# Where the attention masks are added: an identity product on TensorE, or an addition by VectorE in PSUM

## The chip, the cores and the metric

One NeuronCore of a Trainium2 chip runs the whole program. The metric is the device time of one execution in microseconds. It was 2264.13 us as the median of three runs (2263.20 to 2264.96).

## The reference

The input is one sequence of 256 tokens with 1024 features. Two blocks of two layers each follow one another. All arithmetic is fp32. What matters here are the attentions, each of which masks its scores before a softmax:

- Block 1, per layer: a sliding-window attention with sinks, 8 query heads over 2 shared key heads of 64 columns:

```
scores = jnp.where(valid[None, :, None, None], scores, -jnp.inf)
sink = jnp.broadcast_to(sinks..., scores.shape[:-1] + (1,))
probs = jax.nn.softmax(jnp.concatenate([scores, sink], axis=-1), axis=-1)[..., :-1]
```

- Block 2, per layer: a causal latent attention (8 heads, 96 columns per key), and a sparse attention with three branches (compressed keys, selected keys, window) of 8 heads over 2 key heads each:

```
s = jnp.einsum('bthd,bshd->bhts', qi, k).astype(jnp.float32) * scale
s = jnp.where(kpos[None, :] <= qpos[:, None], s, NEG_INF)
p = jax.nn.softmax(s, axis=-1).astype(v.dtype)
```

With 256 tokens all 4 blocks of 64 keys are selected, and the window of 512 covers everything, so that both of those branches are plain causal attentions. A cross-attention of 4 heads per layer has no mask. Block 1 also has a stick-breaking attention, whose mask the change does not touch. The rest are projections, gates and feed-forward products.

## The kernel before

**Products.** Each fp32 product is made from three passes over rounded halves: a weight piece of 1024 columns lands in a ring of 7 slots (SyncE issues the DMA, L380), ScalarE rounds it to `w_high` (L401), VectorE subtracts to get `w_low` (L404), and TensorE multiplies high by high, high by low and low by high. In `gemm_beside` (L602, L603) two instructions do that for 128 features and 256 tokens; one such *gate tile* uses up one weight piece. VectorE then adds the two halves of the bank (L612), and ScalarE applies the gate function (L1462 or L2222). PSUM banks 0 to 3 serve these products.

**Attention units.** The heads of an attention are worked off in units that fill one PSUM bank, 4 or 5 in turn. For query tile t the width of a head is 128 * (t + 1) keys (16 in the compressed branch), and a unit has up to 512 columns. So each attention has, per layer, two units of 4 heads for t = 0 and four units of 2 heads for t = 1; the compressed branch has four units of 4 heads. A unit passes through four engines' instructions:

1. `scores` or `scores_of_two` on TensorE: the mask by an identity product, and a product for each head (L916 or L893); flag `scored`.
2. `maximum` on VectorE: the row maximum (L1036), in block 1 the maximum with the sink (L1044), and its negative (L1040, in block 1 L1048); flag `max_ready`.
3. `exponentials` on ScalarE: for each head an exponential out of the bank (L1090) and a read of the row sum (ACTIVATION_READ_ACCUMULATOR on the same line); flag `p_ready` with the last.
4. `turn_weights` on TensorE: four transposes (L935) into bank 6, after `p_ready` and after the copy of the unit before; `copy` on VectorE (L1059); `values` on TensorE (L951) into bank 7.

**The mask.** It lies in SBUF as bf16, 0 or -1e30. Where a head is 256 wide and `mask_late` is set (all of block 2), the left 128 keys are allowed anyway, so the product only adds the causal triangle to the right half of each head, after the scores (L898, L923; 256 columns). Everywhere else it opens the bank (L888, L911): 512 columns, or 64 in the compressed branch.

**The order beside it** is written out by hand, the same for all engines. The window attention of block 1 and the sparse attention of block 2 are taken two units at a time (`attend_tensor_by_two`, `attend_vector_by_two`): scores of units u and u + 1, values of u - 2, a gate tile or branch product, transposes of u, values of u - 1, another product, transposes of u + 1. VectorE takes both maxima, then the sum of a finished product, a weight piece's `w_low`, the copy of u, and so on. The latent attention is taken one unit at a time (`attend_tensor`): scores of u, transposes of u - 1, one or two gate tiles, values of u - 2. Here VectorE has, between two maxima, one or two gate sums, as many weight pieces, and a slice of side work from a generator (rotations at L1138 to L1144, the short convolution at L2557 to L2575). ScalarE has the weight pieces of the next products (L401) right behind the exponentials of a unit. On each engine the instructions run in the order they are written.

Of the kernel before, what the change touches and what calls it, by code (L numbers as in the profile page):

```python
# [8 lines left out]
ALU = mybir.AluOpType  # L9
# [3 lines left out]
P = 128  # L13
# [262 lines left out]
class Core:  # L276
# [600 lines left out]
    def scores(self, pe, l, u):  # L877
# [5 lines left out]
        region = bank[:, 0:len(heads) * w]  # L883
        mask = a["mask"](t)
        late = mask is not None and w == 2 * P and a["mask_late"]
        started = mask is not None and not late
        if started:
            pe.matmul(region, self.identb[:, :], mask[:, 0:len(heads) * w], start=True, stop=False,  # L888
                      skip_group_check=True)
# [6 lines left out]
        if late:  # L896

            m = pe.matmul(region.rearrange("p (h w) -> p h w", w=w)[:, :, P:w], self.identb[:, :],  # L898
                          self.masks[:, 0, 0:len(heads) * P], start=False, stop=True, skip_group_check=True)
        m.then_inc(*self.flag("scored").one())  # L900

    def scores_of_two(self, pe, l, u):
# [5 lines left out]
        w, mask, late = a["width"](t), a["mask"](t), a["mask_late"] and a["width"](t) == 2 * P  # L908
        if not late:
            for bank, _, _, heads in both:  # L910
                pe.matmul(bank[:, 0:len(heads) * w], self.identb[:, :], mask[:, 0:len(heads) * w], start=True,  # L911
                          stop=False, skip_group_check=True)
        for i in range(len(heads)):
            for bank, _, _, heads in both:
                (q, k), = a["qk"](heads[i], t)
                m = pe.matmul(bank[:, i * w:(i + 1) * w], q, k, start=late and i == 0, stop=True,  # L916
                              skip_group_check=True)
                if not late and i == len(heads) - 1:
                    m.then_inc(*self.flag("scored").one())
        if late:  # L920
            for bank, _, _, heads in both:
                region = bank[:, 0:len(heads) * w].rearrange("p (h w) -> p h w", w=w)
                pe.matmul(region[:, :, P:w], self.identb[:, :], self.masks[:, 0, 0:len(heads) * P], start=False,  # L923
                          stop=True, skip_group_check=True).then_inc(*self.flag("scored").one())
# [104 lines left out]
    def vector_steps(self, dve, l, us, names, finishes):  # L1029
        def maximum(u):  # L1030
# [4 lines left out]
            src = self.psum[:, 4 + u % 2, 0:len(heads) * w].rearrange("p (h w) -> p h w", w=w)  # L1035
# [2042 lines left out]
```

## Time and profile before

| | |
|---|---|
| median of 3 runs | 2264.13 us |
| the profiled execution, its own time | 2265.73 us |
| its span | 2264.0 us |
| ScalarE busy | 1121.6 us (50%) |
| GpSimd busy | 202.4 us (9%) |
| chain that ended last: PE, DVE, ACT, DMA | 96%, 2%, 1%, 1% |
| TensorE clock granted, mean | 0.998 of full |

The span runs from the first to the last instruction that the hardware profiler recorded; the device time has a little around it. In the timeline view each row has a start, a length, the engine, the line and the operation; "[1.93 <-ACT w_high L401]" says that the engine had been idle for 1.93 us and that this instruction released it. TensorE's rows overlap: a matmul's length includes its way through the array, so what it costs the next one is read from start to start. VectorE's rows overlap by some 0.08 us as well when one does not wait for the other.

### The profile page before, as it was taken

The numbers are of one execution on the slowest core, as the hardware profiler recorded it, in microseconds if no ns is written. First come the engines' busy times: TensorE is split into PE (matmuls) and PEld (weight loads), VectorE is DVE, ScalarE is ACT, GpSimd is POOL, SyncE is SP. The second block draws the span as 40 slices with busy tenths as digits, with TensorE's granted clock in tenths as the row PEclk, the third lists the DMA queues.
The fourth block names the chain that finished last, engine by engine and source line by source line (L and its number), as shares of the span: only waits on it lengthen the run. The fifth ranks groups of instructions, "written<-read, shape, count | busy, mean of one in ns | idle before, by whom it ended". The sixth has DMA issues, their size and how long they took to land.

```text
span 2264.0 us, 33433 instructions
## 1 busy us (share of the span) xinstructions
PE 2240.2 (99%) x13314; PEld 1936.3 (86%) x13314; DVE 1552.8 (69%) x2158; ACT 1121.6 (50%) x1737; POOL 202.4 (9%) x192
## 2 busy tenths in 40 slices
PE   8999999999999999999999999999999999999998
PEld 7898888888888888788889988888888888998887
DVE  5677855667864775677777677577655777777764
ACT  4645444554543544545454554454445545455543
POOL 0001200001210210000004001011100000220110
PEclk9999999999999999999999999999999999999999
DMA  6335565434555655554435455565556544364554
GB/s 234 127 134 185 187 203 179 149 122 155 202 192 185 226 193 190 171 184 154 168 103 168 168 205 186 188 222 185 188 172 188 170 154 136 122 214 167 187 191 135
DMA packets 108987, 395.61 MB, mean 175 GB/s; under 512 B 12374, under 2 KB 12544, under 8 KB 108576
## 3 DMA queue, kind: packets, MB, share of 16 engines
q1 hardware_dynamic: 104256, 377.01, 49.7%
q0 software_dynamic: 4576, 16.45, 2.2%
q8 instruction: 107, 1.75, 0.3%
q14 instruction: 48, 0.39, 0.0%
HBM read 392.92 MB, written 1.05 MB: 174 GB/s over the span
## 4 chain that ended last, share of the span: by engine, by line
PE 96%; DVE 2%; ACT 1%; DMA 1%; issue 0%; SPq 0%; DVEq 0%; ACTq 0%
PE psum L447 43%; PE psum L603 28%; PE psum L602 14%; PE psum L951 3%; PE psum L818 2%; PE psum L935 1%; PE psum L916 1%; PE psum L893 1%; PE psum L2039 1%; DMA ring<-in_weights 1%; DVE w_low L404 1%; PE psum L1310 0%; PE psum L1298 0%; DVE x L680 0%; DVE xs L2409 0%
## 5 line engine op out<-in xcount | busy, mean ns | idle before, releaser
L404 DVE TENSOR_TENSOR w_low<-ring,w_high 128x1024 fp32r<-128x1024 f32 x704 | 858.6, 1231 | 351.7 <-ACT w_high L401 349.8
L603 PE MATMUL psum<-xT,w_high 128*128 128x512 f32 x2784 | 980.2, 395 | 0.0
L401 ACT ACTIVATE w_high<-ring 128x1024 fp32r<-128x1024 f32 x704 | 734.6, 1056 | 476.8 <-DMA ring<-in_weights 476.1
L602 PE MATMUL psum<-xT,w_low 128*128 128x256 f32 x2784 | 788.8, 283 | 0.1
L603 PEld LDWEIGHTS psum<-xT,w_high 128*128 128x128 f32 x2784 | 523.0, 188 | 119.1
L602 PEld LDWEIGHTS psum<-xT,w_low 128*128 128x128 f32 x2784 | 526.8, 189 | 1.3 <-issue 0.4
L447 PE MATMUL psum<-w_high,hidden 128*128 128x512 f32 x1216 | 376.9, 390 | 0.0
L447 PEld LDWEIGHTS psum<-w_high,hidden 128*128 128x128 f32 x1216 | 228.2, 188 | 47.2
L447 PE MATMUL psum<-w_low,hidden 128*128 128x512 f32 x608 | 236.6, 389 | 0.0
L447 PE MATMUL psum<-w_high,xT 128*128 128x512 f32 (+2 forms) x640 | 193.2, 383 | 3.7 <-ACT xT L771 1.4
L447 PE MATMUL psum<-rounded_pages,w_high 128*128 128x256 f32 x896 | 165.1, 286 | 0.0
L623 POOL TENSOR_TENSOR hidden<-attn_pT,hidden 128x256 fp32r<-128x256 f32 (+1 forms) x108 | 111.1, 1029 | 580.6 <-ACT hidden L2153 390.2
L447 PEld LDWEIGHTS psum<-w_high,xT 128*128 128x128 f32 x640 | 119.5, 190 | 30.4 <-issue 9.6
L447 PEld LDWEIGHTS psum<-rounded_pages,w_high 128*128 128x128 f32 x896 | 139.4, 191 | 0.5
L447 PEld LDWEIGHTS psum<-w_low,hidden 128*128 128x128 f32 x608 | 114.1, 188 | 23.5
L612 DVE TENSOR_REDUCE attn_p<-psum 128x256 f32<-128x512 f32 x136 | 93.8, 690 | 55.9 <-PE psum L603 54.2
L1090 ACT ACTIVATE attn_p<-psum,nmx 128x256 f32<-128x256 f32 (+2 forms) x176 | 68.3, 401 | 128.4 <-DVE nmx L1040 100.1
L447 PE MATMUL psum<-rounded_pages,w_low 128*128 128x256 f32 x448 | 126.7, 283 | 0.0
L447 PE MATMUL psum<-w_high,rounded_pages 128*128 128x512 f32 x384 | 123.8, 395 | 0.0
L447 PE MATMUL psum<-w_low,xT 128*128 128x512 f32 (+2 forms) x320 | 120.0, 380 | 0.0
L2173 ACT ACTIVATE attn_p<-attn_p 128x256 f32<-128x256 f32 x80 | 33.4, 418 | 136.3 <-DVE attn_p L612 136.2
L612 DVE TENSOR_REDUCE attn_pT<-psum 128x256 f32<-128x512 f32 x80 | 55.3, 691 | 61.8 <-PE psum L603 61.7
(245 smaller groups left out, 2197.4 us busy)
## 6 DMA issues: line engine op xcount, KB each, us to landing
ring<-in_weights SPq DMA_DIRECT2D x706, 512.0 KB, 3.5
pages<-in_affine POOLq DMA_DIRECT2D x16, 512.0 KB, 5.7
ring<-in_weights SPq DMA_DIRECT2D x8, 440.0 KB, 3.1
pages<-in_gains POOLq DMA_DIRECT2D x4, 512.0 KB, 5.1
pages<-in_mem POOLq DMA_DIRECT2D x2, 1024.0 KB, 5.5
ring<-in_weights SPq DMA_DIRECT2D x4, 384.0 KB, 3.1
pages<-in_rows POOLq DMA_DIRECT2D x2, 512.0 KB, 5.9
y<-x SPq DMA_DIRECT2D x4, 256.0 KB, 2.0
```

What stands on the lines that cost most here:

```text
L401: eng.activation(high, raw, ACT.Copy).then_inc(self.flag("w_rounded").sem, 1)
L404: eng.tensor_tensor(self.w_low[:, piece % SLOTS, 0:width], raw, high.bitcast(F32), ALU.subtract).then_inc(self.flag("w_split").sem, 1)
L447: m = pe.matmul(out, a, b, start=(first and i == 0), stop=(last and i == len(pairs) - 1))
L602: pe.matmul(out[:, 0:SEQ], low, self.xT_high[:, k, :], start=(k == 0), stop=False, skip_group_check=True)
L603: m = pe.matmul(out, high, self.xT[:, k, :, :].rearrange("p x s -> p (x s)"), start=False, stop=(k == kn - 1), skip_group_check=True)
L612: dve.tensor_reduce(out, h.rearrange("p (x s) -> p s x", x=2), AX, ALU.add).then_inc(*self.drained(banks, key))
L623: pool.tensor_tensor(low, whole[:, n % (4 // tiles), :], high.bitcast(F32), ALU.subtract).then_inc(*self.flag("hidden").one())
L818: m = pe.transpose(out, src, self.ident[0:n, 0:n])
L893: m = pe.matmul(bank[:, i * w:(i + 1) * w], q, k, start=not started, stop=True, skip_group_check=True)
L951: m = pe.matmul(self.psum[:, 7, h * dv:(h + 1) * dv], self.attn_pT[0:n, u % 2, c * P:(c + 1) * P], a["v"](h, kt), start=(kt == 0), stop=(k ...
L1090: m = act.activation(self.attn_p[:, u % 2, i * w:(i + 1) * w], self.psum[:, 4 + u % 2, i * w:(i + 1) * w], ACT.Exp, bias=self.nmx[:, t, h: ...
L2173: act.activation(silu[:, n % 4, :], silu[:, n % 4, :], ACT.Silu).then_inc(*c.flag("silu").one())
```

## The change

The identity products go; the scores of the first head open the bank instead. VectorE adds the mask to the same columns of the bank in place, ahead of the row maximum, and the maximum waits for it. The `scored` flag is now set by the last score product of each unit. The expected totals of the flag `dve_step` rise by 6 and 22 per layer, one for each masked unit.

```diff
 def scores(self, pe, l, u):
-        region = bank[:, 0:len(heads) * w]
-        mask = a["mask"](t)
-        late = mask is not None and w == 2 * P and a["mask_late"]
-        started = mask is not None and not late
-        if started:
-            pe.matmul(region, self.identb[:, :], mask[:, 0:len(heads) * w], start=True, stop=False,
-                      skip_group_check=True)
+        started = False
...
-        if late:
-            m = pe.matmul(region.rearrange("p (h w) -> p h w", w=w)[:, :, P:w], self.identb[:, :],
-                          self.masks[:, 0, 0:len(heads) * P], start=False, stop=True, skip_group_check=True)
         m.then_inc(*self.flag("scored").one())
...
 def scores_of_two(self, pe, l, u):
-        if not late:
-            for bank, _, _, heads in both:
-                pe.matmul(bank[:, 0:len(heads) * w], self.identb[:, :], mask[:, 0:len(heads) * w], start=True,
-                          stop=False, skip_group_check=True)
...
-                if not late and i == len(heads) - 1:
+                if i == len(heads) - 1:
                     m.then_inc(*self.flag("scored").one())
-        if late:
-            for bank, _, _, heads in both:
-                region = bank[:, 0:len(heads) * w].rearrange("p (h w) -> p h w", w=w)
-                pe.matmul(region[:, :, P:w], self.identb[:, :], self.masks[:, 0, 0:len(heads) * P], start=False,
-                          stop=True, skip_group_check=True).then_inc(*self.flag("scored").one())
...
 def maximum(u):
             src = self.psum[:, 4 + u % 2, 0:len(heads) * w].rearrange("p (h w) -> p h w", w=w)
+            if a["mask"](t) is not None:
+                late = w == 2 * P and a["mask_late"]
+                masked = src[:, :, P:w] if late else src
+                mask = (self.masks[:, 0, 0:len(heads) * P] if late else a["mask"](t)[:, 0:len(heads) * w]
+                        ).rearrange("p (h w) -> p h w", h=len(heads))
+                dve.tensor_tensor(masked, masked, mask, ALU.add).then_inc(*self.flag("dve_step").one())
+                self.settle(dve, l, "dve_step")
             dve.tensor_reduce(self.mx[:, t, hs], src, AX, ALU.max
                               ).then_inc(*self.flag("dve_step").one())
```

**VectorE, first two units of the window attention (block 1, layer 0).** `psum` is the bank of scores, `mx` and `nmx` the maximum and its negative, `w_low` a weight piece, `fac` the sinks' term. Before:

```order
L404 TENSOR_TENSOR w_low<-ring,w_high 128x1024
L1036 TENSOR_REDUCE mx<-psum 128x4
L1044 SCALAR_TENSOR_TENSOR mx<-mx,rows 128x4
L1048 TENSOR_SCALAR nmx<-mx 128x4
L1036 TENSOR_REDUCE mx<-psum 128x4
L1044 SCALAR_TENSOR_TENSOR mx<-mx,rows 128x4
L1048 TENSOR_SCALAR nmx<-mx 128x4
L994 TENSOR_TENSOR fac<-nmx,rows 128x8
```

With the change:

```order
L404 TENSOR_TENSOR w_low<-ring,w_high 128x1024
L1021 TENSOR_TENSOR psum<-psum,masks 128x512
L1023 TENSOR_REDUCE mx<-psum 128x4
L1031 SCALAR_TENSOR_TENSOR mx<-mx,rows 128x4
L1035 TENSOR_SCALAR nmx<-mx 128x4
L1021 TENSOR_TENSOR psum<-psum,masks 128x512
L1023 TENSOR_REDUCE mx<-psum 128x4
L1031 SCALAR_TENSOR_TENSOR mx<-mx,rows 128x4
L1035 TENSOR_SCALAR nmx<-mx 128x4
L974 TENSOR_TENSOR fac<-nmx,rows 128x8
```

One addition stands ahead of each maximum, behind the same weight piece; nothing else moved.

**VectorE, latent attention (block 2, layer 0), units 1 and 2.** The rows between the two maxima are unit 0's copy, two gate sums, two weight pieces and the side work. Before:

```order
L1036 TENSOR_REDUCE mx<-psum 128x4
L1040 TENSOR_SCALAR nmx<-mx 128x4
L1059 COPY attn_pT<-psum 128x512
L612 TENSOR_REDUCE gates<-psum 128x256 x2
L404 TENSOR_TENSOR w_low<-ring,w_high 128x1024 x2
L2557 TENSOR_TENSOR pages<-pages,cols 128x15x16 x2
L1036 TENSOR_REDUCE mx<-psum 128x2
L1040 TENSOR_SCALAR nmx<-mx 128x2
```

With the change:

```order
L1021 TENSOR_TENSOR psum<-psum,masks 128x512
L1023 TENSOR_REDUCE mx<-psum 128x4
L1027 TENSOR_SCALAR nmx<-mx 128x4
L1046 COPY attn_pT<-psum 128x512
L612 TENSOR_REDUCE gates<-psum 128x256 x2
L404 TENSOR_TENSOR w_low<-ring,w_high 128x1024 x2
L2544 TENSOR_TENSOR pages<-pages,cols 128x15x16 x2
L1021 TENSOR_TENSOR psum<-psum,masks 128x2x128
L1023 TENSOR_REDUCE mx<-psum 128x2
L1027 TENSOR_SCALAR nmx<-mx 128x2
```

The copy, the gate sums and the weight pieces come after the first addition, and the second unit's mask has 256 columns.

**TensorE, latent attention, scores of unit 2 and transposes of unit 1.** Before:

```order
L602 MATMUL psum<-xT,w_low 128x256
L603 MATMUL psum<-xT,w_high 128x512
L893 MATMUL psum<-pages 128x256 x2
L898 MATMUL psum<-masks,identb 128x2x128
L935 MATMUL psum<-ident,attn_p 128x128 x4
```

With the change:

```order
L602 MATMUL psum<-xT,w_low 128x256
L603 MATMUL psum<-xT,w_high 128x512
L887 MATMUL psum<-pages 128x256 x2
L915 MATMUL psum<-ident,attn_p 128x128 x4
```

The identity product that stood ahead of the transposes is gone, and the transposes follow the scores directly.

## Rows read from the trace of the kernel before

**Rows 1.** The page: busy time of each engine and its share of the span.
```profile
PE 2240.2 (99%) x13314; PEld 1936.3 (86%) x13314; DVE 1552.8 (69%) x2158; ACT 1121.6 (50%) x1737; POOL 202.4 (9%) x192
```

**Rows 2.** Timeline of TensorE: start, length, then the instruction; mask products and what follows.
```profile
120.44 0.60 PE L911 MATMUL psum<-masks,identb 128*128 128x512 bf16 x2
120.98 1.16 PE L916 MATMUL psum<-pages 64*128 64x128 f32 x16
...
1050.80 0.39 PE L888 MATMUL psum<-masks,identb 128*128 128x512 bf16 x1
1051.03 1.06 PE L893 MATMUL psum<-pages 96*128 96x128 f32 x8
...
1065.55 0.28 PE L898 MATMUL psum<-masks,identb 128*128 128x256 bf16 x1
1065.66 0.64 PE L935 MATMUL psum<-ident,attn_p 128*128 128x128 f32 x4
...
1119.91 0.23 PE L911 MATMUL psum<-masks,identb 128*128 128x64 bf16 x2
1120.08 1.07 PE L916 MATMUL psum<-kcmpT,pages 64*128 64x16 f32 x16
```

**Rows 3.** VectorE's groups by form: count | busy us, mean ns | idle before, releaser.
```profile
L1553 DVE TENSOR_TENSOR x<-x,psum 128x512 f32<-128x512 f32 x16 | 10.9, 682 | 6.1 <-PE psum L447 6.1
...
L2591 DVE TENSOR_TENSOR pages<-pages,psum 128x256 f32<-128x256 f32 x36 | 14.9, 418 | 17.0 <-ACT pages L2201 16.6
```

**Rows 4.** Timeline, window attention of layer 0, unit 0, from weight piece to transposes.
```profile
121.24 1.22 DVE L404 TENSOR_TENSOR w_low<-ring,w_high 128x1024 fp32r<-128x1024 f32 x1
122.38 0.68 DVE L1036 TENSOR_REDUCE mx<-psum 128x4 f32<-128x512 f32 x1
...
124.79 0.21 ACT L1090 ACTIVATION_READ_ACCUMULATOR attn_p<-psum,nmx 128x1 f32 x1
125.06 0.66 PE L935 MATMUL psum<-ident,attn_p 128*128 128x128 f32 x4
```

**Rows 5.** Timeline, latent attention of layer 0: units 0 and 1, then unit 4.
```profile
1057.96 0.21 ACT L1090 ACTIVATION_READ_ACCUMULATOR attn_p<-psum,nmx 128x1 f32 x1
1058.70 0.60 PE L935 MATMUL psum<-ident,attn_p 128*128 128x128 f32 x4
1059.16 2.36 DVE L404 TENSOR_TENSOR w_low<-ring,w_high 128x1024 fp32r<-128x1024 f32 x2 [1.93 <-ACT w_high L401]
1063.16 0.69 DVE L1036 TENSOR_REDUCE mx<-psum 128x4 f32<-128x512 f32 x1
1063.88 0.17 DVE L1040 TENSOR_SCALAR nmx<-mx 128x4 f32<-128x4 f32 x1
1063.96 0.68 DVE L1059 COPY attn_pT<-psum 128x512 f32<-128x512 f32 x1
1064.56 1.28 DVE L612 TENSOR_REDUCE gates<-psum 128x256 f32<-128x512 f32 x2
1065.38 0.22 ACT L1090 ACTIVATION_READ_ACCUMULATOR attn_p<-psum,nmx 128x1 f32 x1
...
1083.48 0.20 ACT L1090 ACTIVATION_READ_ACCUMULATOR attn_p<-psum,nmx 128x1 f32 x1
1083.91 0.60 PE L935 MATMUL psum<-ident,attn_p 128*128 128x128 f32 x4
```

**Rows 6.** Timeline, sparse attention of layer 0, unit 4 of 16 (units 0 to 3 are the compressed branch).
```profile
1143.84 0.21 ACT L1090 ACTIVATION_READ_ACCUMULATOR attn_p<-psum,nmx 128x1 f32 x1
1144.78 0.60 PE L935 MATMUL psum<-ident,attn_p 128*128 128x128 f32 x4
```

**Rows 7.** Stretches: busy us of each engine, granted clock (0.71), DMA share, GB/s; sparse attention, layer 1.
```profile
1895.00:1900.00 5.00, 5.00 (x25) 4.05 (x23) 3.70 (x9) 4.00 (x19) 0.00 (x0) 0.71 0.00 1
```

**Rows 8.** The same view, the latent attention of layer 1 (VectorE's busy time is the third).
```profile
1821.00:1856.00 35.00, 35.00 (x222) 30.95 (x221) 31.37 (x61) 17.89 (x49) 0.00 (x0) 1.00 0.39 130
```

**Rows 9.** Waits of TensorE: who waited for whom, us in total, times, longest.
```profile
PE psum L935 <- ACT attn_p L1090: 2.0, 4, 1.2
```

More of the change, by code:

```diff
@@ L907, in scores_of_two @@
         a, t, heads = self.units[u]
-        w, mask, late = a["width"](t), a["mask"](t), a["mask_late"] and a["width"](t) == 2 * P
-        if not late:
-            for bank, _, _, heads in both:
-                pe.matmul(bank[:, 0:len(heads) * w], self.identb[:, :], mask[:, 0:len(heads) * w], start=True,
-                          stop=False, skip_group_check=True)
+        w = a["width"](t)
         for i in range(len(heads)):
@@ L915, in scores_of_two @@
                 (q, k), = a["qk"](heads[i], t)
-                m = pe.matmul(bank[:, i * w:(i + 1) * w], q, k, start=late and i == 0, stop=True,
-                              skip_group_check=True)
-                if not late and i == len(heads) - 1:
+                m = pe.matmul(bank[:, i * w:(i + 1) * w], q, k, start=i == 0, stop=True, skip_group_check=True)
+                if i == len(heads) - 1:
                     m.then_inc(*self.flag("scored").one())
-        if late:
-            for bank, _, _, heads in both:
-                region = bank[:, 0:len(heads) * w].rearrange("p (h w) -> p h w", w=w)
-                pe.matmul(region[:, :, P:w], self.identb[:, :], self.masks[:, 0, 0:len(heads) * P], start=False,
-                          stop=True, skip_group_check=True).then_inc(*self.flag("scored").one())
     def turn_weights(self, pe, l, u):
@@ L2877 @@
          'drained3': 18,
-         'dve_step': 66,
+         'dve_step': 72,
          'act_step': 4,
@@ L2918 @@
          'drained3': 47,
-         'dve_step': 149,
+         'dve_step': 171,
          'act_step': 8,
```

## The prediction

> **What bounds the kernel now.** I read the page's busy shares first. TensorE is busy 99% of the span, VectorE 69%, ScalarE 50% [rows 1]. So any column taken off TensorE comes off the time, unless TensorE then waits. Whether it waits is decided unit by unit, so the second view is the timeline of the six attention stretches. There I compare two instants for each unit: the end of ScalarE's last accumulator read, which releases the transposes, and the start of the transposes. In the window attention that is 125.00 against 125.06 [rows 4]: a slack of 0.06 us. Where TensorE demonstrably waited, the gap was still 0.05, so usable slack is the gap less 0.05. The third view, the stretches, shows how full VectorE is there: 31.37 of 35 us in a latent attention [rows 8], 90%, far above its average. The change takes work from the engine that bounds the whole and gives three times as much to the one that is nearly full locally, inside the chain scores, maximum, exponential, transposes.
>
> **What is removed.** From start to start, two 512-column identity products cost 0.54 us in the window attention, one costs 0.23 ahead of the latent scores, a 256-column one 0.11, a pair of 64 columns 0.17 [rows 2]. Per layer:
> - window attention, three pairs of 512 columns: about 1.59;
> - latent attention, two of 512 and four of 256: 0.45 + 0.45 = 0.90;
> - sparse attention, two pairs of 64 columns (0.32), two of 512 (1.04) and four of 256 (0.92, each pair as two of the 256-column products): 2.28.
>
> That is 4.77 us a layer, 9.5 us in all for 56 products.
>
> **What is added.** 56 additions on VectorE, 24 of 512 columns, 24 of 256 and 8 of 64. An addition that reads 512 columns of PSUM takes 0.682 us, of 256 columns 0.418 [rows 3]; both write to SBUF. VectorE writing into PSUM stands in no row, so the price is bounded: below by the 0.60 us from one independent 512-column instruction to the next (the copy at 1063.96 and the sum at 1064.56 [rows 5]), above by the 1.22 us of an instruction that handles 1024 columns [rows 4], as if read and write each took a pass. I take the rows of the same shape, 0.69 and 0.42, since input and columns agree. The maximum now waits for the addition; before a wait the next start comes 0.72 us after the maximum's (1063.16 to 1063.88 [rows 5]), so 0.04 more: 0.73, 0.46, and 0.25 for 64 columns (an estimate between 0.46 and nothing, by shape).
> Here a page speaks otherwise. The Trainium skill (VectorE: DVE Perf Modes, "The DRAIN you can't avoid") says that a semaphore after each operation costs nothing extra, as the pipe empties in any case. The trace disagrees: 0.60 without the wait, 0.72 with it. By the page the additions would cost 0.12 less each, and the sum below would be some 1.9 us lower, 2264.8 us.
>
> In total VectorE gets about 30 us more. Off the chain that costs nothing: outside the attentions it is not loaded further, and the second unit of each pair has 2.3 us of slack or more nearly everywhere.
>
> **Where TensorE will wait.** I follow each stretch with two shifts against before: of the exponentials' end and of TensorE. The rows of one unit stand for each kind; the other slacks were read alike.
>
> *Window attention.* Unit 0's maximum starts at 122.38 behind a weight piece that began at 121.24 [rows 4] and waits on ScalarE, not on the scores. So the exponentials end 0.73 later while TensorE comes 0.54 earlier: wait 0.73 + 0.54 - 0.01 = 1.26. The later pairs have 1.61 of slack against at most 0.73 + 0.53; no wait. Net per layer 1.26 - 1.59 = **-0.33**.
>
> *Latent attention.* Slacks of the six units: 0.53, 0.06, 2.04, 1.12, 0.23, 1.27. After unit 0's exponentials (end 1058.17) ScalarE rounds two pieces, VectorE was idle for 1.93 us until the first, splits both, does side work and only then takes unit 1's maximum at 1063.16; its exponentials end at 1065.60, TensorE turns at 1065.66 [rows 5, 2]. So exponentials, weight pieces, side work and next maximum form a loop over ScalarE and VectorE with hardly a gap, and each addition shifts all that follows: the shifts of the exponentials are 0.73, 1.46, 1.92, 2.38, 2.84, 3.30. TensorE against them:
> - unit 0: 0.45 earlier, usable 0.48, wait 0.70, TensorE at +0.25;
> - unit 1: one product less (+0.14), usable 0.01, wait 1.31, at +1.45;
> - unit 2: at +1.34, no wait; unit 3: +1.23, usable 1.07, wait 0.08;
> - unit 4: exponentials ended at 1083.68, turned at 1083.91 [rows 5]; +1.20, usable 0.18, wait 1.46, at **+2.66**;
> - unit 5: 3.30 against 2.66 + 1.22, no wait.
>
> Layer 1 has nearly the same slacks (0.53, 0.07, 1.94, 1.02, 0.24, 1.25) and gives +2.65.
>
> *Sparse attention.* Layer 0 begins with slacks 0.05, 0.05 (a wait already), 0.17: waits 0.42, 0 and 0.28. Unit 4 [rows 6] has 0.94 less its last accumulator's 0.21, so 0.73; VectorE is busy without a gap from unit 2's exponentials on: exponentials +1.23, TensorE -0.14, wait 0.69. Units 6 and 8 have 1.64: none. Unit 10 has 0.96 against 0.73 + 0.52: wait 0.34. Units 12 and 14 have 1.10: none. Waits 1.73, net **-0.55**. Layer 1 has more slack (1.06, 0.05, 1.71, 3.78, 1.42): waits 0.42 and 0.35, net **-1.52**.
>
> **Sum.** 2 x -0.33 + 2.66 + 2.65 - 0.55 - 1.52 = +2.6 us: 12.1 us of new waits against 9.5 us removed. The profiled execution took 2265.73, 1.6 us above the median of 2264.13; the sum changes neither in kind, so I forecast 2264.1 + 2.6 = **2266.7 us**, 0.11% above. A measurement of this kernel can tell about 0.2%, 4.5 us, from no change.
>
> **Rivals.**
> 1. *All covered.* TensorE never waits, all 9.5 us come back: 2254.6. For it: usable slack of 1.5 to 3.5 us in most pairs. Against it: 0.06, 0.53, 0.06, 0.23 in [rows 4, 5] are smaller than one addition. 0.10.
> 2. *The shifts do not add up.* Were the loop reset by TensorE or the DMA at each unit, only units 0, 1 and 4 would wait, 0.70, 0.83 and 0.39, and a latent layer would give +1.03: 2264.1 - 0.7 = 2263.4. For it: VectorE idles 1.93 us once [rows 5]. Against: that idle time ends with ScalarE, which was itself behind the exponentials. 0.24.
> 3. *Slower: writing PSUM is dear.* If an addition takes 1.22 us for 512 columns and 0.27 more for 256, a latent layer loses 2 x 0.53 + 3 x 0.27 = 1.9 more, a window layer 0.7, the sparse attentions 1.6 together: 2266.7 + 6.8 = 2273.5. It decides from 0.15 us above my price on. For it: no row shows such a write. Against: in [rows 3] an instruction that touches PSUM takes what its columns ask. 0.10.
> 4. *The clock.* In layer 1's sparse attention TensorE was granted 0.71 on average over 5 us [rows 7], both levels (1.2 and 2.4 GHz) in one stretch, behind narrow products of the compressed branch; that costs 5 x 0.29 = 1.5 us. Layer 0 shows no such fall. The new waits sit in the same places. One more fall gives 2268.2, two more 2269.7; slower by over 0.2% with the top of my own range. Without the one that is there: 2265.2. The Trainium skill (TensorE: Matmul & The Clock Gate, "A second HAM failure mode") says that frequent short idling between groups of matmuls makes the clock swing; [rows 7] bear it out once. 0.08 for two or more.
>
> That the change does not do what it says is excluded by the order of instructions.
>
> **Chances.** My forecast has 0.48. Faster by over 0.2% is rival 1 and a small part of rival 2: 0.14. Slower is rivals 3 and 4 and the top of my forecast, where VectorE's delay also holds up gate sums or `w_low`: 0.24. Within: 0.62. The range goes from 2259 (rival 2 with the lower price and no fall of the clock) to 2271 (forecast with half of rival 3's surcharge): it leaves out most of rival 1 and half of rival 3.
>
> **What would show it.** TensorE's list of waits should name the exponentials with some 12 us in about twelve places, where it named 2.0 us in 4 [rows 9]. The transposes of latent units 1 and 4 should come 1.4 and 2.7 us later against the stretch's first scores. The addition's row should read 0.69 us for 512 columns; above 0.84 rival 3 holds. If the latent stretch grows by 1 us rather than 2.7, rival 2 does. If TensorE shows under 5 us of waits, I was wrong about the loop altogether.

## The result, and the profile after

The median is 2270.5 us over ten executions (2266.73 to 2273.79), against 2264.41 us for the kernel before beside it (2262.13 to 2268.31). The ratio is **1.0026**, 95% interval [1.0016, 1.0036]: slower by 0.26%, a little more than the 0.2% that can be told apart. A later set on another chip (five executions, median 2272.64 us) gave 1.0042 [1.0029, 1.0054]. One further execution of the kernel before, of 3165 us at a granted clock of 0.654, is left out of all figures. The profiled execution took 2266.73 us itself, the fastest of the ten, with a span of 2265.0 us. On the lines of the new kernel: L1021 is the addition, L1023 the maximum, L1077 the exponentials, L915 the transposes, L931 the values.

The page's busy times, which answer to [rows 1]:
```profile
PE 2233.0 (99%) x13258; PEld 1931.4 (85%) x13258; DVE 1579.1 (70%) x2214; ACT 1120.6 (49%) x1737; POOL 201.9 (9%) x192
```
TensorE has 56 instructions and 7.2 us less, VectorE 56 instructions and 26.3 us more, and the time is not shorter.

VectorE's groups by form, where [rows 3] had only the neighbours of the addition (count | busy us, mean ns | idle before):
```profile
L1021 DVE TENSOR_TENSOR psum<-psum,masks 128x512 f32<-128x512 f32 x24 | 16.6, 691 | 0.0
...
L1021 DVE TENSOR_TENSOR psum<-psum,masks 128x64 f32<-128x64 f32 x8 | 1.8, 221 | 0.0
```
The addition in PSUM takes 0.691 us for 512 columns and 0.221 for 64; 256 columns took 0.435 (24 of them, 10.4 us). Writing to PSUM is no dearer here than reading it: 0.682 and 0.418 stood in [rows 3].

The waits of TensorE, which answer to [rows 9]:
```profile
PE psum L915 <- ACT attn_p L1077: 7.8, 13, 1.1
...
PE psum L931 <- DVE pages L2461: 1.6, 2, 0.8
```
Before it was 2.0 us in 4 places. The second row is new: the values of a latent unit wait until VectorE has emptied bank 7.

The window attention's unit 0, timeline, which answers to [rows 4]:
```profile
122.17 0.69 DVE L1021 TENSOR_TENSOR psum<-psum,masks 128x512 f32<-128x512 f32 x1
122.89 0.69 DVE L1023 TENSOR_REDUCE mx<-psum 128x4 f32<-128x512 f32 x1
...
125.31 0.21 ACT L1077 ACTIVATION_READ_ACCUMULATOR attn_p<-psum,nmx 128x1 f32 x1
125.58 0.66 PE L915 MATMUL psum<-ident,attn_p 128*128 128x128 f32 x4 [1.03 <-ACT attn_p L1077]
```
Addition to maximum is 0.72 us from start to start, as the forecast had it. The transposes started 0.06 us after the exponentials before; now TensorE stands idle for 1.03 us ahead of them.

TensorE in the latent attention of layer 0, which answers to [rows 5]:
```profile
1049.97 1.05 PE L887 MATMUL psum<-pages 96*128 96x128 f32 x8
...
1058.11 0.66 PE L915 MATMUL psum<-ident,attn_p 128*128 128x128 f32 x4 [0.55 <-ACT attn_p L1077]
...
1066.25 0.66 PE L915 MATMUL psum<-ident,attn_p 128*128 128x128 f32 x4 [1.06 <-ACT attn_p L1077]
...
1083.65 1.08 PE L931 MATMUL psum<-pages,attn_pT 128*128 128x64 f32 x8 [0.79 <-DVE pages L2461]
...
1085.88 0.66 PE L915 MATMUL psum<-ident,attn_p 128*128 128x128 f32 x4 [0.23 <-ACT attn_p L1077]
```
Before, from the start of the first unit's mask product (1050.80 in [rows 2]) to unit 4's transposes (1083.91 in [rows 5]) there were 33.11 us; now there are 35.91 from the first scores: 2.80 more. To unit 1's transposes it was 14.86 us and is 16.28, 1.42 more. The forecast had 2.7 and 1.4. On VectorE in the same stretch:
```profile
1059.04 2.36 DVE L404 TENSOR_TENSOR w_low<-ring,w_high 128x1024 fp32r<-128x1024 f32 x2 [1.92 <-ACT w_high L401]
...
1063.04 0.69 DVE L1021 TENSOR_TENSOR psum<-psum,masks 128x512 f32<-128x512 f32 x1
...
1067.18 2.36 DVE L404 TENSOR_TENSOR w_low<-ring,w_high 128x1024 fp32r<-128x1024 f32 x2 [0.73 <-ACT w_high L401]
...
1070.29 0.49 DVE L1021 TENSOR_TENSOR psum<-psum,masks 128x256 f32<-128x256 f32 x1
...
1073.74 2.36 DVE L404 TENSOR_TENSOR w_low<-ring,w_high 128x1024 fp32r<-128x1024 f32 x2 [0.24 <-ACT w_high L401]
```
Each pair of low halves still waits for ScalarE's rounding, which stands behind the exponentials, which stand behind the addition. That is the loop.

**Where the time went, stretch by stretch.** For each stretch I took the distance in time between the same two products (L447 or L603) at its ends in both profiled executions; the differences, after less before, in us:

| stretch | forecast | measured |
|---|---|---|
| window attention, layers 0 and 1 | -0.33, -0.33 | -0.13, -0.17 |
| latent attention, layers 0 and 1 | +2.66, +2.65 | +2.77, +2.90 |
| sparse attention, layers 0 and 1 | -0.55, -1.52 | -0.44, -1.50 |
| three feed-forward stretches | 0 | -1.79, -1.78, +1.80 |
| all else (the rest of the difference of the spans) | 0 | -0.66 |
| sum | +2.6 | +1.0 |

The feed-forward stretches are in code that the change does not touch; they are taken up at the end. Without them and the rest the measured terms give +3.4 us. In the sparse attentions the table also holds one fall of TensorE's clock, in layer 1 before and in layer 0 after, which is taken up with the prediction.

### The profile page after: what moved, and what is told of

It reads as the page before. It is cut to its first block, busy times and chain, and to the rows that moved or that the text cites. A ratio compares the mean times of both kernels' runs of the same rounds, so it can differ in the third digit from the quotient of the medians.

```text
span 2265.0 us, 33377 instructions
## 1 busy us (share of the span) xinstructions
PE 2233.0 (99%) x13258; PEld 1931.4 (85%) x13258; DVE 1579.1 (70%) x2214; ACT 1120.6 (49%) x1737; POOL 201.9 (9%) x192
## 3 DMA queue, kind: packets, MB, share of 16 engines
HBM read 392.92 MB, written 1.05 MB: 174 GB/s over the span
## 4 chain that ended last, share of the span: by engine, by line
PE 92%; DVE 5%; ACT 2%; issue 1%; DMA 0%; DVEq 0%; SPq 0%; ACTq 0%
PE psum L447 42%; PE psum L603 27%; PE psum L602 14%; PE psum L931 2%; PE psum L818 2%; DVE w_low L404 2%; PE psum L915 1%; ACT attn_p L1077 1%; PE psum L902 1%; PE psum L2026 1%; ACT w_high L401 1%; PE psum L1297 0%; PE psum L1285 0%; DVE mx L1023 0%; PE psum L887 0%
## 5 line engine op out<-in xcount | busy, mean ns | idle before, releaser
L603 PE MATMUL psum<-xT,w_high 128*128 128x512 f32 x2784 | 978.4, 395 | 0.0
L603 PEld LDWEIGHTS psum<-xT,w_high 128*128 128x128 f32 x2784 | 522.7, 188 | 117.4
L447 PE MATMUL psum<-w_high,hidden 128*128 128x512 f32 x1216 | 376.8, 390 | 0.0
L447 PEld LDWEIGHTS psum<-w_high,hidden 128*128 128x128 f32 x1216 | 228.3, 188 | 47.3
L447 PE MATMUL psum<-w_low,hidden 128*128 128x512 f32 x608 | 236.6, 389 | 0.0
L447 PE MATMUL psum<-w_high,xT 128*128 128x512 f32 (+2 forms) x640 | 192.9, 383 | 3.6 <-ACT xT L771 1.4
L447 PE MATMUL psum<-rounded_pages,w_high 128*128 128x256 f32 x896 | 165.1, 286 | 0.0
L447 PEld LDWEIGHTS psum<-w_high,xT 128*128 128x128 f32 x640 | 119.2, 190 | 30.1 <-issue 9.4
L447 PEld LDWEIGHTS psum<-rounded_pages,w_high 128*128 128x128 f32 x896 | 139.4, 191 | 0.5
L1077 ACT ACTIVATE attn_p<-psum,nmx 128x256 f32<-128x256 f32 (+2 forms) x176 | 68.0, 399 | 137.1 <-DVE nmx L1027 109.1
L447 PEld LDWEIGHTS psum<-w_low,hidden 128*128 128x128 f32 x608 | 114.2, 188 | 23.5
L447 PE MATMUL psum<-rounded_pages,w_low 128*128 128x256 f32 x448 | 126.7, 283 | 0.0
L447 PE MATMUL psum<-w_high,rounded_pages 128*128 128x512 f32 x384 | 123.8, 395 | 0.0
L447 PE MATMUL psum<-w_low,xT 128*128 128x512 f32 (+2 forms) x320 | 119.7, 379 | 0.0
```

The source lines that it names most:

```text
L447: m = pe.matmul(out, a, b, start=(first and i == 0), stop=(last and i == len(pairs) - 1))
L603: m = pe.matmul(out, high, self.xT[:, k, :, :].rearrange("p x s -> p (x s)"), start=False, stop=(k == kn - 1), skip_group_check=True)
L1077: m = act.activation(self.attn_p[:, u % 2, i * w:(i + 1) * w], self.psum[:, 4 + u % 2, i * w:(i + 1) * w], ACT.Exp, bias=self.nmx[:, t, h: ...
```

## Experiments

All were timed alternating with the kernel before, in four sets, each on a chip of its own. "Stretch" figures below are against the first profile of the kernel before, made as in the table above.

| run | median us | ratio to before | latent, layers 0 and 1 |
|---|---|---|---|
| before_again | 2264.66 | 1.0005 [0.9994, 1.0016] | -0.13, +0.03 |
| after_again | 2272.64 | 1.0042 [1.0029, 1.0054] | +2.81, +2.87 |
| no_masks | 2260.11 | 0.9991 [0.9982, 0.9999] | -0.14, -0.13 |
| both_ways | 2271.56 | 1.0045 [1.0032, 1.0059] | +2.77, +2.94 |
| latent_only | 2268.65 | 1.0027 [1.0015, 1.0038] | +2.75, +2.91 |
| paired_only | 2261.57 | 0.9998 [0.9989, 1.0007] | -0.10, +0.03 |
| loop_opened | 2262.95 | 1.0001 [0.9991, 1.0012] | +0.44, +0.43 |
| where_covered | 2263.23 | 0.9996 [0.9987, 1.0005] | +0.34, +0.43 |
| latent_twice | 2278.62 | 1.0065 [1.0052, 1.0079] | +5.66, +5.78 |
| order_alone | 2262.41 | 0.9996 [0.9987, 1.0005] | -0.19, -0.06 |
| later_tiles_only | 2262.18 | 0.9991 [0.9982, 1.0000] | 0.00, +0.04 |
| narrow_kept | 2267.14 | 1.0021 [1.0011, 1.0031] | +2.79, +2.93 |

### The two kernels once more

> The kernel before, unchanged, taken again for its granted clock in every run. Theory A (TensorE's clock falls more often with the change: 2270.5 us against 2266.7 forecast): the mean granted clock of its runs is 0.998 to 0.999, one fall or none, and runs near 2264 us; ratio 0.999 to 1.001. Theory B (the added time is the same waits in every run, and the clock has no part): its granted clocks are spread as those of the changed kernel are (0.996 to 0.999).

> The changed kernel, unchanged, taken again. Theory A: granted clocks of 0.996 to 0.998, each 0.001 worth 2.3 us, the ratio 1.002 to 1.003, and the profile shows two to four stretches at half clock outside the end, in the attention stages. Theory B: the profile shows one or none, and the time is still near 2270, from longer waits of TensorE for the exponentials than the 12 us forecast.

The kernel before against itself gives 1.0005, so the comparison holds to 0.1%. The granted clocks settle neither theory: 0.997 to 0.999 in the kernel before (mean 0.9981 over 11 executions), 0.996 to 0.999 in the change (0.9976 over five). The latent stretch of the change came out within 0.04 us of its first profile. Most of what differs between the two profiles of the change, 7.7 us, lay elsewhere: 4.3 us in the sparse attentions, where the clock fell for longer, 1.8 us net in the feed-forward stretches, 0.5 us between the two window attentions.

### Neither products nor additions

```diff
-            if a["mask"](t) is not None:
...
-                dve.tensor_tensor(masked, masked, mask, ALU.add).then_inc(*self.flag("dve_step").one())
-                self.settle(dve, l, "dve_step")
```

> The changed kernel without VectorE's additions: the shared-key and latent attentions of both blocks are computed without any mask. Prices the term 'removed' alone. Forecast: 9.5 us less than before, 2254.6 to 2255.2, ratio 0.9958. If the clock falls more often because the identity products are gone, and not because of the waits, its clocks are below those of before and the ratio is 0.997 or more.

This is what the removed products are worth alone, and the 9.5 us expected were wrong: the time fell by about 2 us. The expectation had left out the slacks that the forecast itself lists. The window stretches gained 0.85 and 0.88 us where products of 1.59 were counted, the latent stretches 0.14 and 0.13 where 0.90 went. TensorE waited for the exponentials already, and a product ahead of a wait is free: in the latent attention nearly all of them were.

Part of the shortfall is the price of the products themselves. In the window attention, from the transposes to the next scores, first before, then without masks:
```profile
128.35 0.60 PE L935 MATMUL psum<-ident,attn_p 128*128 128x128 f32 x4
...
129.31 1.14 PE L916 MATMUL psum<-pages 64*128 64x256 f32 x8
```
```profile
129.22 0.60 PE L915 MATMUL psum<-ident,attn_p 128*128 128x128 f32 x4
129.75 1.13 PE L902 MATMUL psum<-pages 64*128 64x256 f32 x8
```
And in the sparse attention, from scores to the gate tile behind the values:
```profile
1149.76 1.13 PE L916 MATMUL psum<-pages 64*128 64x256 f32 x8
...
1151.87 0.36 PE L602 MATMUL psum<-xT,w_low 128*128 128x256 f32 x1
```
```profile
1149.73 1.14 PE L902 MATMUL psum<-pages 64*128 64x256 f32 x8
...
1151.71 0.36 PE L602 MATMUL psum<-xT,w_low 128*128 128x256 f32 x1
```
A pair of 512 columns is worth 0.96 less 0.53, 0.43 us, and a pair of 256 columns 2.11 less 1.98, 0.13 us; the forecast had 0.53 and 0.23. The products around them lose part of what goes. With the masks left out altogether and the order of the work as it is, the gain is 0.1% (interval 0.0 to 0.2%), which bounds a change of this kind in this order.

### Products and additions together

```diff
 def maximum(u):
+            if a["mask"](t) is not None:
...
+                dve.tensor_tensor(masked, masked, mask, ALU.add).then_inc(*self.flag("dve_step").one())
+                self.settle(dve, l, "dve_step")
             dve.tensor_reduce(self.mx[:, t, hs], src, AX, ALU.max
```

> The kernel before with VectorE's additions on top: masks are added twice, which leaves the weights at zero where they were. Prices the waits while TensorE keeps its products. TensorE then arrives 9.5 us later in all, so the waits should be smaller than 12.1 us: window layers 0.73 each, latent layers 2.5 each, sparse 0.7 and 0.3, 8 us in all if the shifts add up along the loop of ScalarE and VectorE (latent stretch +2.5 us each by its rows), 4 us if they do not (latent stretch +1). Ratio 1.0035 against 1.0015; more falls of the clock come on top, 1.5 us each.

The window stretches lost 0.73 and 0.69 us, the price of one addition with its wait: with the 0.86 of the run above this makes the -0.13 of the change. The latent stretches lost 2.77 and 2.94, as much as the change itself; 2.5 was expected. Keeping the identity products there made no difference; the addition alone does it.

### The two halves of the change

```diff
+    def on_vector(self, u):
+        a, t, heads = self.units[u]
+        return a["mask"](t) is not None and (a["name"] == "mla")
```
(and `!=` for the other; a unit for which it is false keeps its identity product and gets no addition)

> VectorE adds the mask in the latent attention alone; the other masks stay identity products. Theory A (delays add up along the loop exponentials, rounded pieces, low pieces, side work, next maximum): each latent stretch is 2.7 to 2.9 us longer than before, as in the changed kernel, 5.6 us in all, ratio 1.0025, nearly the whole loss of the change. Rival (each unit waits for itself): +1.0 per stretch, ratio 1.001. Of the clock: if its falls come with the waits of the compressed branch, this kernel's clocks are those of before.

> VectorE adds the masks in the window and sparse attentions, taken two units at a time; the latent attention keeps its identity products. Theory A: window stretches -0.2 each, sparse -1.3 and 0 us without falls of the clock, 2 us less than before in all, ratio 0.999; with the changed kernel's extra falls of the clock in the compressed branch (1.5 us each) the gain is gone, ratio 1.000. Rival (VectorE's load does harm everywhere alike): a part of the loss in proportion to the additions, 44 of 56, ratio 1.002.

The latent attentions, 12 of the 56 additions, carry the loss. The 44 others together can't be told from no change; their rival's 1.002 lies outside the interval. Waits of TensorE, first with the additions in the latent attention alone:
```profile
PE psum L945 <- ACT attn_p L1107: 6.0, 11, 1.1
```
and with those of the window and sparse attentions alone:
```profile
PE psum L945 <- ACT attn_p L1107: 4.1, 7, 1.0
```
The second adds waits as well, 2.1 us over the kernel before, but has removed products that did cost time.

### The addition made twice

```diff
-                dve.tensor_tensor(masked, masked, mask, ALU.add).then_inc(*self.flag("dve_step").one())
-                self.settle(dve, l, "dve_step")
+                for _ in range(2):
+                    dve.tensor_tensor(masked, masked, mask, ALU.add).then_inc(*self.flag("dve_step").one())
+                    self.settle(dve, l, "dve_step")
```

> Additions of the latent attentions alone, each made twice in a row (the second changes no masked score that matters, but costs VectorE the same time again); window and sparse attentions as before. It measures the slope of the loop. Theory (exponentials, low halves, side work and next maximum form a closed loop, so each addition shifts all that follows): the shifts of the exponentials double to 1.46, 2.92, 3.84, 4.76, 5.68, 6.60 us; with the slacks and the removed products of the forecast TensorE leaves the stretch at +5.5 us per layer against before, where one addition gave +2.8. Time about before + 11, ratio 1.005. Rival A (the loop is reset at each unit): +1.1 us per layer. Rival B (what costs is one more handshake per unit, whatever its length, or the missing identity product that used to cover the wait): +2.8 to +3.5 us per layer, as with one addition.

+5.66 and +5.78 us per layer, where the loop gave +5.5 and a loop reset at each unit +1.1. TensorE's rows, for those shown above of the change:
```profile
1050.04 1.05 PE L895 MATMUL psum<-pages 96*128 96x128 f32 x8
...
1058.94 0.66 PE L945 MATMUL psum<-ident,attn_p 128*128 128x128 f32 x4 [1.31 <-ACT attn_p L1108]
...
1067.82 0.66 PE L945 MATMUL psum<-ident,attn_p 128*128 128x128 f32 x4 [1.81 <-ACT attn_p L1108]
...
1088.84 0.66 PE L945 MATMUL psum<-ident,attn_p 128*128 128x128 f32 x4 [0.70 <-ACT attn_p L1108]
```
First scores to unit 4's transposes is 38.80 us: 33.11 before, 35.91 with one addition, 38.80 with two. A second addition costs as much again as the first did, as a closed loop has it; that rules out rival B, by which one more step or the missing product would cost and not its length. The ratio is higher than expected, 1.0065 for 1.005: the two stretches make 11.4 us of the 14.6 between the medians, and where the rest lies these four executions don't show.

### The loop opened

In the latent attention VectorE writes the low halves one unit later, so that a unit's maximum no longer stands behind pieces that ScalarE rounds after the exponentials before it.

```diff
-            waiting = [6]
+            waiting, behind = [6], []
...
-                waiting[:] = BESIDE_MLA.get(i, [])
-                for n in waiting:
+                for n in behind:
                     split(gate_split(n))
+                waiting[:] = BESIDE_MLA.get(i, [])
+                behind[:] = waiting
                 next(side, None)
```

> The changed kernel, but in the latent attention VectorE makes the low half of the weight pieces one unit later, behind the next maximum, so that no maximum waits behind pieces that ScalarE rounds after the last exponentials. No arithmetic changes. Theory A: the loop is cut; each latent stretch loses its 2.8 us and comes to 0 to 0.9 us below before, ratio 1.0000 to 1.0015 against the changed kernel's 1.003. Rival (VectorE is simply full there, 90% busy): the same instructions in another order, the stretch stays 2 to 2.8 us above before.

> The kernel before (identity products, no additions) with VectorE's low halves of the latent attentions written one unit later, as in the run with the opened loop. Theory: with no addition in it the loop already kept up with TensorE except for slacks of 0.05 to 0.2 us at a few units, so this order gains nothing in the latent stretch (-0.2 to 0 us per layer, which is what leaving out masks altogether gave there: -0.14) or loses where a low half now comes late for its gate tile (up to +0.4, which is what remained with the additions in the opened loop). Ratio to before 0.999 to 1.001. Rival: the old order itself cost TensorE something; then this kernel gains 1 us or more per layer and the addition in the opened loop is not free but was paid for by the order.

With all 56 additions, the same kernel in this order is level with the kernel before: 1.0001 instead of 1.0026 to 1.0042. The stretches are 0.44 and 0.43 us above before, where 0 to 0.9 below was expected; in layer 0 TensorE still waits 0.56 us ahead of unit 0's transposes and 0.37 ahead of unit 5's. The order by itself gains nothing (-0.19 and -0.06 us per latent stretch), so what it gives back with the additions, 2.3 to 2.5 us per layer, is the loop's. One view shows it for the four kernels: 35 us of layer 0's latent attention, with the busy time of PE, PEld, DVE, ACT and POOL, the granted clock, the DMA share and GB/s. Before:
```profile
1055.00:1090.00 35.00, 35.00 (x223) 30.90 (x222) 31.30 (x60) 17.55 (x49) 0.00 (x0) 1.00 0.40 133
```
The change:
```profile
1055.00:1090.00 35.00, 32.23 (x199) 27.63 (x198) 31.32 (x60) 17.49 (x48) 0.00 (x0) 1.00 0.37 120
```
The additions made twice:
```profile
1055.00:1090.00 35.00, 29.30 (x178) 25.02 (x178) 31.21 (x60) 15.99 (x43) 0.00 (x0) 1.00 0.36 119
```
The loop opened:
```profile
1055.00:1090.00 35.00, 34.07 (x213) 30.04 (x212) 32.13 (x60) 18.11 (x49) 0.00 (x0) 1.00 0.38 124
```
TensorE's idle time is 0, 2.77, 5.70 and 0.93 us. VectorE's busy time is the same in the first three (31.2 to 31.3): an instruction put in pushes others out of the 35 us. It is not full, though: the new order raises it, to 32.1, which speaks against the rival that VectorE has no room left. VectorE's rows in it:
```profile
1060.87 0.69 DVE L1021 TENSOR_TENSOR psum<-psum,masks 128x512 f32<-128x512 f32 x1
...
1064.19 2.35 DVE L404 TENSOR_TENSOR w_low<-ring,w_high 128x1024 fp32r<-128x1024 f32 x2
...
1067.45 0.43 DVE L1021 TENSOR_TENSOR psum<-psum,masks 128x256 f32<-128x256 f32 x1
...
1070.51 2.35 DVE L404 TENSOR_TENSOR w_low<-ring,w_high 128x1024 fp32r<-128x1024 f32 x2
...
1075.20 0.43 DVE L1021 TENSOR_TENSOR psum<-psum,masks 128x256 f32<-128x256 f32 x1 [1.44 <-PE psum L887]
```
The low halves no longer wait for `w_high`, and the addition waits for TensorE's scores: VectorE runs ahead.

### Additions only where they are covered

```diff
-        return a["mask"](t) is not None and (a["name"] == "mla")
+        return a["mask"](t) is not None and (t == 1 and a["name"] in ("swa", "slc", "win"))
```
(later_tiles_only, set against latent_only; where_covered also has the latent additions, in the opened loop)

> Masks by VectorE only where the rows showed cover: window attention and the two causal branches of the sparse one at query tile 1, and the latent attention with the low halves one unit later as in loop_opened; the first units of each pair at tile 0 and the compressed branch keep their identity products. Theory A: -1.06 per window stretch, -0.9 per latent, -0.9 per sparse, 5.7 us in all, ratio 0.9975, with the clock as before. Rival (removed products do not come back, since exponentials are late anyway, as in no_masks): -2 to -3 us, ratio 0.999.

> Additions only in the units of the second query tile of the window attention and of the selected and window branches of the sparse attention, identity products elsewhere: the places where the forecast's slacks cover an addition. Theory: window stretch -0.85 us per layer as without any mask, latent 0, second half of the sparse stretch -0.4, sum -2 to -3 us over the program, ratio 0.9985 to 1.0. Rival: the sum is eaten by clock falls in the compressed branches (0 to 2 per layer, 1.5 us each, in every kernel alike), and the ratio cannot be told from 1.

For where_covered 5.7 us less was expected, for later_tiles_only 2 to 3. The window stretches gave -0.81 and -0.89, then -0.83 and -0.89 us: all that no_masks had. The second half of the sparse attentions gave -0.49 and -0.37. The times are 0.9996 and 0.9991 of before. So the 5.7 us were wrong and the rival of 2 to 3 us is nearer: removed products do not come back where TensorE waits anyway, and the latent stretches of where_covered even stayed 0.3 to 0.4 us above before. The second kernel is the best of those with their masks in place and level with having none, but 0.1% is less than can be told from no change here.

### Which additions go with the falls of the clock

```diff
-        return a["mask"](t) is not None and (a["name"] == "mla")
+        return a["mask"](t) is not None and a["name"] != "cmp"
```
(set against latent_only again; against the change, the compressed branch has its identity products back)

> The change everywhere except in the compressed branch, whose units of 16 columns a head keep their identity products (64 columns each) and get no addition. It asks what makes the clock fall there more often with the change: the granted clock was 0.9983 on average over 60 executions of the kernel before and 0.9975 over 15 of the change, a difference of 1.8 us. Theory: the falls come with gaps and narrow products in the compressed branch itself, and the additions there lengthen the gaps; then this kernel goes back to 0.9982 to 0.9984, its time is 2 us below the change's, ratio to before 1.0015 to 1.003, and the latent stretch stays at +2.8 us per layer. Rival: the falls depend on when TensorE arrives there, not on these additions (the kernels with additions in that branch and an opened or absent latent loop had 0.9984 and 0.9979); then the mean clock stays at 0.9975 and the ratio at 1.003 to 1.004. Second rival: the difference of the clocks is chance; then nothing can be told apart.

The mean granted clock was 0.9986 over 12 executions, against 0.9975 over 15 of the change (and 0.9985 over 17 of the kernel before in the same set). The mean time was 4.7 us above the kernel before of the same set, where the change's 15 executions were 7.4 us above the kernel before in all sets, and the latent stretches are unchanged. That is the outcome of the theory, but its ratio, 1.0021 [1.0011, 1.0031], can't be told from the first 1.0026 of the change, and other kernels disagree about the cause:

- the same additions in the compressed branch: 0.9984 in the opened loop (11 executions), 0.9979 in paired_only (11);
- no additions there, but TensorE just as late: 0.9984 in latent_only (7);
- neither products nor additions: 0.9978 in no_masks (11).

Single executions of the kernel before scatter by 0.0008, so means over 7 to 12 of them scatter by 0.0002 to 0.0003. What makes the falls more frequent stays open.

## Why the prediction was right, and where it was short

**Level, not faster.** The forecast's core was that the engine with most of the busy time would not profit, and it did not: 2266.7 was forecast, 0.11% above, and 0.26% was measured, inside the range but on the slower side of the 0.2%, to which I gave 0.24. It is inside by 0.5 us only (2270.5 against 2271), and the median of the second set, 2272.64, is outside. The mechanism, the loop in the latent attention, is what the runs bear out; that the number fell inside owes something to luck, as follows.

**Removed, 9.5 us.** This term was too large. The 0.23 and 0.11 us of the single products in the latent attention hold, but pairs are worth 0.43 and 0.13 us, not 0.53 and 0.23, and the 64-column pairs 0.07, not 0.16. That makes 3.7 us a layer instead of 4.77, some 7.5 us in all, so new waits of about 11 us rather than 12.1 give the +3.4 that was measured. Their worth was mostly taken care of by the slacks: with no addition the forecast's rule gives -1.05 for a window and -0.3 for a latent stretch; measured were -0.86 and -0.14.

**Added.** 0.691, 0.435 and 0.221 us against 0.69, 0.42 and 0.21 to 0.25: right. The wait adds 0.04 (0.72 from start to start) as read before. The Trainium skill (VectorE: DVE Perf Modes, "The DRAIN you can't avoid") says that a semaphore after each operation cost nothing extra in its test; the same section adds that an instruction which is not held starts earlier. The trace has the second case: 0.72 with the wait against the 0.60 without it in [rows 5]. Rival 3 is refuted.

**Window attention.** -0.33 forecast, -0.15 measured. The term that was off is the products of the later pairs: 1.05 forecast, 0.86 measured; the addition's 0.73 was exact (0.73 and 0.69 in both_ways).

**Latent attention.** +2.66 and +2.65 forecast, +2.77 and +2.90 measured. The shifts add up; rival 2, which gave +1.03, is refuted by latent_only and by the slope of latent_twice. One detail was wrong: of unit 4's wait a large part (0.79 of 1.02) is not for the exponentials but for VectorE's L2461, which empties bank 7 and stands just ahead of unit 4's addition in VectorE's order. It is late by the same shifts: it comes 2.51 us later than before against the stretch's start (1082.81 less 1049.97, against 1081.13 less 1050.80), where the forecast has 2.38 for unit 3's exponentials. The forecast had named late side work only as a tail.

**Sparse attention.** -2.07 forecast for both layers, -1.94 measured, and this agreement is luck. The one fall of the clock lay in layer 1 before and in layer 0 after. From the starts of the same products, it cost 1.4 us in layer 0 and its absence gave back 1.8 us in layer 1. Without the falls the layers come to about -1.9 and +0.3 (an estimate), where -0.55 and -1.52 were forecast. Two things were off. The removed products were taken at 2.28 us a layer and measure about 1.5. And layer 0 was read from an execution in which TensorE waited 1.23 us in the compressed branch, ahead of the transposes at 1128.78; in before_again that wait is 0.5 us shorter with the same kernel. That the fall could wander without its number changing had not been considered.

**TensorE's list of waits** names 7.4 us more than before (with the row for L2461), not 12.1. It counts from the end of the last product, which itself takes 0.6 us, so it shows less than the delay: 2.80 us of delay and 0.90 of removed products stand against 2.77 of idle time in the latent stretch. The threshold of 5 us was passed, the figure of 12 a mistake, for the most part in what the view counts.

**The missing 3.5 us.** The medians differ by 6.1 us. The forecast's terms were short by 0.8 us (3.4 against 2.6). The larger part fits rival 4. The granted clock, 0.9983 on average before (100 executions), is 0.9975 with the change (15): 0.0008 of 2264 us, 1.8 us, somewhat more than one fall per execution at 1.5 us. With a scatter of 0.0008 between executions that is more than chance gives, but what brings it about is open, as said above. I gave two or more further falls 0.08 and none a term in the sum, because one profiled execution showed one fall. An event that comes in some executions only can't be sized from one. What is left of the 6.1 us, 0.9, is within the interval of the ratio, 2.3 us either way. By the means of all executions the difference is 7.4 us, and by the second set about 9.5; by those 2 to 4 us are not accounted for.

## What to carry to other kernels

Before moving work off the busiest engine, find the units in which that engine already waits: work ahead of a wait is worth nothing, and an experiment that leaves the work out altogether gives the ceiling at once (here 0.1%). Price the work by what its neighbours gain when it goes, not by its own row: here pairs of products gave 0.1 us less each. On the receiving engine look for a closed loop with another engine: inside one, each instruction's length adds up over all turns, and the remedy that worked here is the order of the work (low halves one unit later). Place the moved work where the next consumer has slack for it, unit by unit.

## What the runs showed of the hardware that was not expected

**The clock falls in the compressed branch in every version, at times that change.** Stretches of the sparse attention of layer 0, columns as above, first the kernel before:
```profile
1125.00:1130.00 5.00, 3.77 (x33) 3.05 (x31) 3.85 (x5) 5.00 (x16) 0.00 (x0) 1.00 0.53 190
1130.00:1133.00 3.00, 3.00 (x25) 2.72 (x25) 2.96 (x6) 1.01 (x2) 0.00 (x0) 1.00 0.10 38
1133.00:1137.00 4.00, 4.00 (x27) 3.38 (x26) 2.74 (x5) 3.98 (x19) 0.00 (x0) 1.00 0.30 112
```
The same kernel in its second profile:
```profile
1125.00:1130.00 5.00, 4.30 (x39) 3.60 (x37) 3.89 (x6) 5.00 (x15) 0.00 (x0) 0.98 0.61 202
1130.00:1133.00 3.00, 3.00 (x12) 2.69 (x12) 2.93 (x8) 0.99 (x8) 0.00 (x0) 0.50 0.02 8
1133.00:1137.00 4.00, 4.00 (x15) 2.97 (x14) 2.38 (x3) 3.58 (x14) 0.00 (x0) 0.55 0.00 0
```
And the change:
```profile
1125.00:1130.00 5.00, 4.43 (x29) 3.49 (x28) 4.22 (x6) 5.00 (x15) 0.00 (x0) 1.00 0.35 110
1130.00:1133.00 3.00, 3.00 (x31) 2.59 (x29) 2.31 (x3) 2.00 (x3) 0.00 (x0) 0.92 0.54 178
1133.00:1137.00 4.00, 4.00 (x18) 3.36 (x17) 2.90 (x10) 2.72 (x13) 0.00 (x0) 0.63 0.00 0
```
0.50 is the lower level (1.2 GHz), 1.00 the higher (2.4 GHz). Every one of the 14 profiles taken shows such a fall in the sparse attention of at least one layer. The kernel before shows none in layer 0 in one execution and seven us at the lower level in the next, and the one without a fall had TensorE busy for less of the stretch ahead (3.77 us of 5, against 4.30 and 4.43). The Trainium skill (TensorE: Matmul & The Clock Gate, "A second HAM failure mode") describes a clock that swings where groups of products (bf16, 512 columns in its case) are separated by short idle times. The place agrees, for the fp32 products of 16 columns here: a stretch with 0.6 to 1.2 us idle in 5; but in these three the one with the most idle time is the one that kept its clock, so the rule tells where to look and not when it happens.

**One stretch of code has two paces at full clock.** A feed-forward stretch of layer 0 in block 2, before and then after:
```profile
1505.00:1620.00 115.00, 115.00 (x651) 99.68 (x650) 86.63 (x106) 60.13 (x86) 22.06 (x27) 1.00 0.63 211
```
```profile
1505.00:1620.00 115.00, 115.00 (x661) 100.97 (x660) 87.61 (x106) 61.26 (x87) 22.62 (x28) 1.00 0.63 216
```
TensorE is never idle and its clock is 1.00 in both, yet it got through 651 products in one and 661 in the other. From the same first to the same last product at L603 there it is 111.74 or 109.96 us, nothing between, in all 14 profiles; the second profile of the kernel before has 109.96. Two other feed-forward stretches do the same, 113.15 or 111.35. That makes 1.8 us each, independent of the change. With the falls it accounts for 6.1 of the 7.7 us between the two profiles of the change. What picks the pace was not found, nor tried. It is one reason why a sum of terms in one profile (+1.0 us here) can differ from the medians (+6.1 us) by more than any of the terms.
